# Expert loop of a two-block kernel: rows gathered and turned for two experts at a time, small matmuls in four groups, the last chunk of gate and up unsplit

## The chip, the cores and the metric

The kernel runs on one core of a Trainium2 chip. Times are microseconds (us) of device time for one execution. The core has TensorE (PE; the loading of its stationary operand is listed as PEld), VectorE (DVE), ScalarE (ACT), GpSimd (POOL) and SyncE (SP), and 16 DMA engines. The metric is the time of the whole kernel.

## The reference

The input is 512 tokens of width 1024 in fp32. A first block runs a gated convolution and a forgetting attention, then a mixture of experts; a second block runs a chunkwise mLSTM with pooling and a latent attention. The change touches the mixture of experts alone:

```python
def hier_moe(h, w_router_group, w_router_expert, w_e_gate, w_e_up, w_e_down):
    # per token: the best of 4 groups, then the best 2 of its 8 experts, with weights
    ...
    x_rows = hf[row_tok].reshape(n_blocks, MOE_BLOCK, D)

    def expert_block(args):
        xb, e = args
        a = xb @ w_e_gate[e]
        u = xb @ w_e_up[e]
        return (jax.nn.silu(a) * u) @ w_e_down[e]
```

There are 32 experts. Gate and up are 1024x512, down is 512x1024, each 2 MB in fp32. The 512 tokens give 1024 rows in all, 32 per expert on average.

## The kernel before

Each engine runs its own program; semaphores order them. Everything outside the experts is the same in both kernels.

**Precision.** Products run as fp32r matmuls on split operands. ACT copies a weight into an fp32r tile (`gate_hi`, `up_hi`, `down_hi`), DVE subtracts it from the weight (`gate_lo`, `up_lo`, `down_lo`, L2257, in place of the loaded weight), each in two halves of 128x2048. The tokens of an expert, at most 64 (`CAP`), are the stationary operand `xs`, with the high parts in columns 0 to 63 and the low parts in columns 64 to 127. For each of the 8 chunks of 128 input features PE runs `xs` against the high and against the low weights (N = 512), into one bank (L1658 and L1659 for gate, L1615 and L1616 for up).

**Sums.** The two halves of rows of a product are added, and turned at once, by 8 small plain fp32 matmuls against `twice` (L1634), after ACT has copied the banks to `g_sb` and `u_sb`. silu, the product `hx` (DVE L2281), its split into `hxs` and the down product (L1682) follow; ACT and DVE add its two halves to `ys` (L2292), and POOL scatters the rows to `y_dram`.

**Rows.** POOL gathers an expert's 64 rows from `h2_dram` into `xg[p]` with an indirect DMA (L771), by a column of `table` that it first copies into `get_row[p]` (L782). Unused places hold an index out of bounds. PE turns them with 8 transposes (L1588) into bank 0, and ACT (`x_high`) and DVE (`x_low`, L2276) split them into `xs[p]`.

**Order.** `period(e, p)` is written out for each engine, with p = e mod 2, and loops run over pairs of experts. On PE it is gate of e, among whose chunks the sums of e - 1 and the turning of the rows of e + 1 are spread one by one, then up of e, then down of e - 1. On ACT: silu of e - 1, first half of gate_hi of e + 1, hxs of e - 1, g_sb of e, x_high of e + 1, second half of gate_hi, u_sb of e, up_hi of e + 1, y_low of e - 1, down_hi of e. On DVE: hx and hxs of e - 1, first half of gate_lo of e + 1, x_low of e + 1, second half, up_lo of e + 1, ys of e - 1, down_lo of e. POOL waits for the turned rows of e + 1, gathers those of e + 3 and scatters those of e - 1.

**Loads.** Gate, up and down have two buffers each (`ring_gate` and so on). SP asks for gate of e + 2 when gate of e is done (`next_gate`, L644), in the same way for up (L648) and, one period later, for down (L652). All go through one queue. The high tiles have one buffer only, so ACT starts gate_hi of e + 1 when gate of e is done.

After expert 31 POOL gives `moe_done` when the last scatter has landed, SP loads the rows of `y_dram` back, and the second block begins.

Of the kernel before, what the change touches and what calls it, by code (L numbers as in the profile page):

```python
# [37 lines left out]
CAP = 64  # L38
TOPK = 2
# [177 lines left out]
def build_kernel(nc, t):  # L217

    with ExitStack() as ctx:
# [14 lines left out]
        bank = [ctx.enter_context(nc.psum_tensor(f"bank{i}", [P, 512], F32)) for i in range(8)]  # L234
# [32 lines left out]
        get_row = [misc(f"get_row{p}", [CAP, 1], I32) for p in range(2)]  # L267
# [59 lines left out]
        xg = [at(f"xg{p}", [CAP, D], F32, BASE + 2 * BIG + 4096 * p) for p in range(2)]  # L327
# [251 lines left out]
        gathered = [sem(f"gathered{p}") for p in range(2)]  # L579
# [10 lines left out]
        half_rows = lambda x: slice(64 * x, 64 * x + 64)  # L590

# [148 lines left out]
        def _(pool):  # L740
# [18 lines left out]
            for p in range(2):  # L759
                step(nc.gpsimd.memset(ys[p][:, :], 0.0))  # L760
                if p == 1:
                    step(nc.gpsimd.memset(xg[p][:, :], 0.0))
                pool.dma_start(y_dram[TOPK * SEQ:, :], ys[p][:, :]).then_inc(scattered, 16)
                pool.wait_ge(scattered, 16 * (p + 1))
# [5 lines left out]
            def gather(p):  # L770
                pool.indirect_dma_start(out=xg[p][:, :], out_offset=None, in_=h2_dram,  # L771
                                        in_offset=bass.IndirectOffsetOnAxis(ap=get_row[p][:, :], axis=0),
                                        bounds_check=SEQ - 1, oob_is_err=False).then_inc(gathered[p], 16)
# [6 lines left out]
            def get(e, p):  # L780

                nc.gpsimd.tensor_copy(get_row[p][:, :], table[:, bass.ds(each(e, 1), 1), 0]).then_inc(sem("get_ready"), 1)  # L782
                pool.wait_ge(sem("get_ready"), each(e, 1, 1))
                pool.sem_inc(turn, 1)
                gather(p)
# [11 lines left out]

            get((None, 0), 0)
            get((None, 1), 1)
            for e in range(2):  # L800
                pool.wait_ge(x_turned, e + 1)
                get((None, e + 2), e)
            with pool.Fori(0, NE // 2 - 1) as i:
                for k in range(2):
                    e, p = (i, 1 + k), (1 + k) % 2
                    pool.wait_ge(x_turned, each(e, 1, 2))
                    pool.sem_inc(turn, 1)
                    get(expert(e, 3), 1 - p)
                    put(expert(e, -1), 1 - p)
            for e in range(NE - 2, NE):  # L810
                put((None, e), e % 2)
            for p in range(2):
                pool.wait_ge(gathered[p], 16 * (NE // 2 + 1))
# [4 lines left out]
            with pool.If(count > 0):  # L818
                with pool.Fori(0, OVF) as i:
                    with pool.If(count > i):  # L820
                        pool.wait_ge(sem("ovf_free"), i + 1)
                        pool.sem_inc(turn, 1)
                        nc.gpsimd.tensor_copy(get_row[0][:, :], table[:, bass.ds(i + NE, 1), 0]).then_inc(sem("ovf_rows"), 1)
# [5 lines left out]
                        pool.indirect_dma_start(out=xg[0][:, :], out_offset=None, in_=h2_dram,  # L829
                                                in_offset=bass.IndirectOffsetOnAxis(ap=get_row[0][:, :], axis=0),  # L830
# [26 lines left out]
        def _(act):  # L857
# [197 lines left out]
            def gate_high(e, p, half):  # L1055
# [3 lines left out]
                cs = slice(half * KC // 2, (half + 1) * KC // 2)  # L1059
                copy(gate_hi[:, cs, :], ring_gate[p][:, cs, :]).then_inc(gate_hi_made, 1)  # L1060

            def up_high(e, p):
                act.wait_ge(up_done, each(e, 1))
                act.wait_ge(up_landed[p], each((e[0], e[1] - p), 8, 16))
                for half in range(2):
                    cs = slice(half * KC // 2, (half + 1) * KC // 2)
# [9 lines left out]
            def x_high(e, p):  # L1076
                act.wait_ge(x_turned, each(e, 1, 1))
                copy(xs[p][:, :, 0:CAP], bank[0][:, :].rearrange("p (c n) -> p c n", c=KC)).then_inc(x_hi_made, 1)
# [273 lines left out]
        def _(pe):  # L1352
# [233 lines left out]
            def turn_row(p, c):  # L1586
                rows = xg[p][:, :].rearrange("t (p c) -> t c p", c=KC)
                return pe.transpose(bank[0][:, c * CAP:(c + 1) * CAP], rows[:, c, :], ident[0:CAP, 0:CAP])  # L1588

            def turn_rows(p, done):  # L1590
# [1117 lines left out]
```

## Time and profile before

| | |
|---|---|
| runs | 1952.59 us median of 3 (1952.17 to 1953.96) |
| the profiled execution | 1952.4 us, of which the span is 1950.6 us |
| mean granted TensorE clock | 0.967 |
| PE busy | 1821.7 us, 93% of the span |
| PEld busy | 1490.4 us, 76% |
| DVE busy | 1199.7 us, 62% |
| ACT busy | 1003.1 us, 51% |
| POOL busy | 334.2 us, 17% |
| DMA | 326.49 MB, mean 167 GB/s |

The span runs from the first instruction to the last; the execution's own time has 1.8 us more around it. The expert loop lies between about 642 and 1185 us of the span. Ends of matmuls are modelled, so the starts of two of them say more than a duration. A share of busy DMA engines can come out a little above 1, since packets of two queues overlap on an engine. A line number is that of the kernel before; L866 is ACT's copy helper.

### The profile page before, as it was taken

The numbers are of one execution on the slowest core, as the hardware profiler recorded it, in microseconds if no ns is written. First come the engines' busy times: TensorE is split into PE (matmuls) and PEld (weight loads), VectorE is DVE, ScalarE is ACT, GpSimd is POOL, SyncE is SP. The second block draws the span as 40 slices with busy tenths as digits, with TensorE's granted clock in tenths as the row PEclk, the third lists the DMA queues.
The fourth block names the chain that finished last, engine by engine and source line by source line (L and its number), as shares of the span: only waits on it lengthen the run. The fifth ranks groups of instructions, "written<-read, shape, count | busy, mean of one in ns | idle before, by whom it ended". The sixth has DMA issues, their size and how long they took to land.

```text
span 1950.6 us, 23766 instructions
## 1 busy us (share of the span) xinstructions
PE 1821.7 (93%) x8894; PEld 1490.4 (76%) x8894; DVE 1199.7 (62%) x1641; ACT 1003.1 (51%) x1332; POOL 334.2 (17%) x191
## 2 busy tenths in 40 slices
PE   7999999999898799999999993989999998999898
PEld 6888878888787577777777772868778887878467
DVE  3442435455554899999999995652548633327453
ACT  4222244444513689898989883445333223438331
POOL 0000000000000155555555540100001000000000
PEclk9999999999999799999999996989999999999799
DMA  7755447433146799999999973323022422213001
GB/s 145 104 91 93 107 74 65 70 57 62 44 142 240 277 406 405 403 405 402 403 402 404 401 280 113 113 72 107 1 87 87 152 87 81 87 46 106 6 1 65
DMA packets 129364, 326.49 MB, mean 167 GB/s; under 512 B 8448, under 2 KB 84992, under 8 KB 121088
## 3 DMA queue, kind: packets, MB, share of 16 engines
q1 hardware_dynamic: 123408, 315.85, 50.4%
q0 software_dynamic: 5440, 8.93, 1.4%
q8 instruction: 57, 0.93, 0.2%
q10 hardware_dynamic: 432, 0.56, 0.1%
q14 instruction: 27, 0.22, 0.0%
HBM read 319.02 MB, written 15.21 MB: 171 GB/s over the span
## 4 chain that ended last, share of the span: by engine, by line
PE 60%; DVE 22%; issue 12%; ACT 4%; DMA 1%; DVEq 0%; POOL 0%; SPq 0%; POOLq 0%; ACTq 0%
PE bank L1355 16%; PE bank L1357 15%; PE bank L1356 15%; DVE gate_lo L2257 5%; DVE down_lo L2257 5%; DVE up_lo L2257 4%; PE bank L1431 2%; DVE ys L2292 2%; PE bank L1526 2%; PE bank L1441 1%; PE bank L1882 1%; ACT w_hi L866 1%; PE bank L1797 1%; DVE xs L2276 1%; PE bank L1881 1%
## 5 line engine op out<-in xcount | busy, mean ns | idle before, releaser
L1910 DVE TENSOR_TENSOR w_lo<-w_raw,w_hi 128x2048 fp32r<-128x2048 f32 (+2 forms) x83 | 179.5, 2164 | 341.5 <-ACT w_hi L866 341.3
L866 ACT ACTIVATE w_hi<-w_raw 128x2048 fp32r<-128x2048 f32 (+3 forms) x139 | 182.2, 1332 | 280.8 <-PE bank L1357 81.5
L1355 PE MATMUL bank<-h1T_hi,w_hi 128*128 128x512 f32 x456 | 183.4, 402 | 0.0
L1357 PE MATMUL bank<-h1T_hi,w_lo 128*128 128x512 f32 x456 | 179.4, 393 | 0.0
L1356 PE MATMUL bank<-h1T_lo,w_hi 128*128 128x512 f32 x456 | 178.7, 392 | 0.0
L793 POOL COPY put_row<-table 64x1 int32 (+1 forms) x32 | 122.3, 3823 | 175.7 <-DVE ys L2292 173.5
L2257 DVE TENSOR_TENSOR gate_lo<-gate,gate_hi 128x2048 fp32r<-128x2048 f32 x64 | 146.0, 2284 | 0.0
L2257 DVE TENSOR_TENSOR up_lo<-up,up_hi 128x2048 fp32r<-128x2048 f32 x64 | 143.6, 2285 | 1.1 <-ACT up_hi L866 1.1
L2257 DVE TENSOR_TENSOR down_lo<-down,down_hi 128x2048 fp32r<-128x2048 f32 x62 | 138.8, 2276 | 0.0
L866 ACT ACTIVATE gate_hi<-gate 128x2048 fp32r<-128x2048 f32 x64 | 122.4, 1914 | 9.3 <-DMA h_dram<-h_tok 9.3
L1658 PE MATMUL bank<-gate_hi,xs 128*128 128x512 f32 x248 | 120.2, 485 | 0.9 <-DVE gate_lo L2257 0.9
L866 ACT ACTIVATE up_hi<-up 128x2048 fp32r<-128x2048 f32 x64 | 119.1, 1920 | 0.0
L866 ACT ACTIVATE down_hi<-down 128x2048 fp32r<-128x2048 f32 x62 | 114.9, 1904 | 0.0
L1355 PE MATMUL bank<-h2T_hi,w_hi 128*128 128x512 f32 x264 | 103.0, 390 | 3.3 <-DVE hy_t L2467 2.2
L1615 PE MATMUL bank<-up_hi,xs 128*128 128x512 f32 x256 | 104.7, 409 | 0.0
L1357 PE MATMUL bank<-h2T_hi,w_lo 128*128 128x512 f32 x264 | 102.7, 389 | 0.0
L1356 PE MATMUL bank<-h2T_lo,w_hi 128*128 128x512 f32 x264 | 102.7, 389 | 0.0
L1616 PE MATMUL bank<-up_lo,xs 128*128 128x512 f32 x256 | 101.5, 396 | 0.0
L1357 PEld LDWEIGHTS bank<-h1T_hi,w_lo 128*128 128x128 f32 x456 | 86.1, 189 | 18.5
L1355 PEld LDWEIGHTS bank<-h1T_hi,w_hi 128*128 128x128 f32 x456 | 87.0, 191 | 16.3
L1356 PEld LDWEIGHTS bank<-h1T_lo,w_hi 128*128 128x128 f32 x456 | 86.4, 189 | 16.6
L1659 PE MATMUL bank<-gate_lo,xs 128*128 128x512 f32 x248 | 98.1, 395 | 0.0
(490 smaller groups left out, 4351.5 us busy)
## 6 DMA issues: line engine op xcount, KB each, us to landing
gate<-in_w_e_gate SPq DMA_DIRECT2D x32, 2048.0 KB, 12.3
up<-in_w_e_up SPq DMA_DIRECT2D x32, 2048.0 KB, 14.5
down<-in_w_e_down SPq DMA_DIRECT2D x32, 2048.0 KB, 16.1
w_raw<-in_w_in SPq DMA_DIRECT2D x24, 1024.0 KB, 9.8
w_raw<-in_a_w_in SPq DMA_DIRECT2D x20, 1024.0 KB, 5.2
w_raw<-in_w_in SPq DMA_DIRECT2D x16, 512.0 KB, 9.6
w_raw<-in_a_w_out SPq DMA_DIRECT2D x8, 1024.0 KB, 4.9
w_raw<-in_c_w_in SPq DMA_DIRECT2D x6, 1024.0 KB, 5.3
```

The lines of the kernel that those rows point to most:

```text
L793: nc.gpsimd.tensor_copy(put_row[p][:, :], table[:, bass.ds(each(e, 1), 1), 1]).then_inc(sem("put_ready"), 1)
L866: return nc.scalar.activation(out, in_, ACT.Copy, scale=scale)
L1355: pe.matmul(out, sh, mh, start=start, stop=False)
L1356: pe.matmul(out, sh, ml, start=False, stop=False)
L1357: return pe.matmul(out, sl, mh, start=False, stop=stop)
L1431: ins = pe.transpose(out[0:src.shape[-1], at_:at_ + n], src, ident)
L1615: pe.matmul(out[:, :], x[:, c, :], wh[:, c, :], start=c == 0, stop=False)
L1616: ins = pe.matmul(out[:, :], x[:, c, :], wl[:, c, :], start=False, stop=c == KC - 1)
L1658: pe.matmul(bank[2][:, :], xs[p][:, c, :], gate_hi[:, c, :], start=c == 0, stop=False)
L1659: ins = pe.matmul(bank[2][:, :], xs[p][:, c, :], gate_lo[p][:, c, :], start=False, stop=c == KC - 1)
L1910: V.tensor_tensor(ring_view(w_lo, n), ring_view(raw, n), ring_view(w_hi, n).bitcast(F32), ALU.subtract)\
L2257: V.tensor_tensor(lo[:, cs, :], raw_[:, cs, :], hi[:, cs, :].bitcast(F32), ALU.subtract).then_inc(lo_made_, 1)
```

## The change

1. **Rows by pairs.** `xg` and `get_row` become one tile of 128 partitions each, for two experts: 0 to 63 for the even one, 64 to 127 for the odd one. One indirect DMA gathers both. PE turns the pair with 8 transposes of 128x128 (`turn_pair`) into a tile of two banks, `turned`, in every other period (p = 1); `turned_of(x)` is the view of one expert's columns. ACT and DVE still split the rows of one expert per period. POOL waits once per pair, gathers the pair after next, and then scatters two experts' outputs.
2. **Small matmuls in four groups.** In `gate_among` the sums, and the transposes where there are any, follow every second chunk, two at a time, in place of one after each chunk.
3. **Last chunk unsplit.** Chunk 7 of gate and up (`SPLIT_KC` = 7) is no longer split. The second halves of gate_hi, up_hi, gate_lo and up_lo cover 3 chunks of 4, and PE runs one plain fp32 matmul against the loaded weight in place of two fp32r ones. down is as before.

```diff
+SPLIT_KC = KC - 1
...
+        turned = ctx.enter_context(nc.psum_tensor("turned", [P, 1024], F32))
+        bank = [turned[:, 512 * (i // 3):512 * (i // 3) + 512] if i in (0, 3)
...
+        turned_of = lambda x: turned[:, :].rearrange("p (c n) -> p c n", c=KC)[:, :, half_rows(x)]
...
+            def get_pair(e):
+
+                for x in range(2):
+                    nc.gpsimd.tensor_copy(get_row[half_rows(x), :], table[:, bass.ds(each(expert(e, x), 1), 1), 0])\
+                        .then_inc(sem("get_ready"), 1)
+                pool.wait_ge(sem("get_ready"), each(e, 1, 2))
                 pool.sem_inc(turn, 1)
-                gather(p)
+                gather()
...
+            get_pair((None, 0))
+            pool.wait_ge(x_turned, 1)
+            get_pair((None, 2))
             with pool.Fori(0, NE // 2 - 1) as i:
+                pool.wait_ge(x_turned, i + 2)
+                pool.sem_inc(turn, 1)
+                get_pair((i, 4))
                 for k in range(2):
...
+                    put((i, k), k)
...
-                cs = slice(half * KC // 2, (half + 1) * KC // 2)
+                cs = slice(half * KC // 2, min(half * KC // 2 + KC // 2, SPLIT_KC))
...
+                if p == 0:
+                    act.wait_ge(x_turned, e[1] // 2 + 1 if e[0] is None else e[0] + (e[1] // 2 + 1))
+                copy(xs[p][:, :, 0:CAP], turned_of(p)).then_inc(x_hi_made, 1)
...
+            def turn_pair(c):
+                rows = xg[:, :].rearrange("t (p c) -> t c p", c=KC)
+                return pe.transpose(turned[:, c * P:(c + 1) * P], rows[:, c, :], ident)
...
+            def row_product(out, x, wh, wl, w, c, e, low_made):
+
+                if c % (KC // 2) == 0:
+                    pe.wait_ge(low_made, each(e, 2, 1 + c // (KC // 2)))
+                if c >= SPLIT_KC:
+                    return pe.matmul(out[:, :], x[:, c, :].bitcast(F32), w[:, c, :], start=False, stop=c == KC - 1)
+                pe.matmul(out[:, :], x[:, c, :], wh[:, c, :], start=c == 0, stop=False)
+                return pe.matmul(out[:, :], x[:, c, :], wl[:, c, :], start=False, stop=c == KC - 1)
...
+                    ins = row_product(bank[2], xs[p], gate_hi, gate_lo[p], ring_gate[p], c, e, gate_lo_made)
                     if c == KC - 1:
                         ins.then_inc(gate_done, 1)
...
+                    if c == 1:
                         sum_waits(expert(e, -1))
...
+                        if turn_next:
+                            turn_waits(expert(e, 1))
+                    if c % 2 == 1:
+                        for k in (c - 1, c):
+                            ins = sum_of(k)
...
+                        if turn_next:
+                            for k in (c - 1, c):
+                                ins = turn_pair(k)
...
             def period(e, p):
-                gate_among(e, p)
+                gate_among(e, p, turn_next=p == 1)
...
+            pe.wait_ge(gathered, 16)
+            for c in range(KC):
+                ins = turn_pair(c)
+            ins.then_inc(x_turned, 1)
             gate_product((None, 0), 0)
-            turn_x((None, 1), 1)
             up_both((None, 0), 0)
...
-                cs = slice(half * n, half * n + n)
+                cs = slice(half * n, min(half * n + n, SPLIT_KC))
```

## Rows read from the trace of the kernel before

**Rows 1.** Stretches: length; busy us of PE, PEld, DVE, ACT, POOL; clock; DMA; GB/s

```profile
660.00:692.40 32.40, 31.47 (x141) 24.64 (x140) 31.29 (x21) 28.98 (x27) 8.09 (x5) 1.00 0.93 354
692.40:1114.70 422.30, 422.30 (x1873) 332.91 (x1873) 409.70 (x287) 384.92 (x352) 242.42 (x106) 1.00 1.01 403
1131.00:1150.40 19.40, 19.40 (x87) 15.43 (x86) 18.92 (x14) 17.32 (x16) 11.61 (x6) 1.00 0.72 292
1164.80:1171.60 6.80, 6.80 (x25) 5.93 (x25) 4.45 (x4) 2.17 (x3) 0.00 (x0) 0.50 0.42 136
```

**Rows 2.** DMA queues in 692.4 to 1114.7: packets, MB, share of 16 engines

```profile
q1 hardware_dynamic: 21165, 163.32, 96.4%
q0 software_dynamic: 4160, 6.89, 5.0%
```

**Rows 3.** Two gate loads and the next to last down load: issue, and us to landing

```profile
L644 SPq DMA_DIRECT2D gate<-in_w_e_gate x1: 351/351/351, 671.5 to 671.5; - x1
DMA to landing us min/median/max: 8.6/8.6/8.6
...
L644 SPq DMA_DIRECT2D gate<-in_w_e_gate x1: 338/338/338, 1126.0 to 1126.0; - x1
DMA to landing us min/median/max: 14.6/14.6/14.6
...
L652 SPq DMA_DIRECT2D down<-in_w_e_down x1: 379/379/379, 1134.2 to 1134.2; - x1
DMA to landing us min/median/max: 16.2/16.2/16.2
```

**Rows 4.** Groups by line in 692.4 to 1114.7: busy us, mean ns, idle before

```profile
L2257 DVE TENSOR_TENSOR gate_lo<-gate,gate_hi 128x2048 fp32r<-128x2048 f32 x53 | 121.0, 2284 | 0.0
...
L866 ACT ACTIVATE gate_hi<-gate 128x2048 fp32r<-128x2048 f32 x53 | 101.5, 1914 | 0.0
...
L2276 DVE TENSOR_TENSOR xs<-bank,xs 128x512 fp32r<-128x512 f32 x26 | 17.8, 684 | 0.0
```

**Rows 5.** DVE in order of time, one expert: start, length, line

```profile
848.28 4.48 DVE L2257 TENSOR_TENSOR down_lo<-down,down_hi 128x2048 fp32r<-128x2048 f32 x2
...
864.52 4.47 DVE L2257 TENSOR_TENSOR down_lo<-down,down_hi 128x2048 fp32r<-128x2048 f32 x2
...
869.81 0.43 DVE L2286 TENSOR_TENSOR hxs<-hx,hxs 128x256 fp32r<-128x256 f32 x1 [0.48 <-ACT hxs L866]
```

**Rows 6.** PE in order of time: gate steps with a turn, then in the last gate

```profile
863.19 0.50 PE L1658 MATMUL bank<-gate_hi,xs 128*128 128x512 f32 x1
...
864.27 0.50 PE L1658 MATMUL bank<-gate_hi,xs 128*128 128x512 f32 x1
...
1151.51 0.48 PE L1658 MATMUL bank<-gate_hi,xs 128*128 128x512 f32 x1
...
1152.20 0.48 PE L1658 MATMUL bank<-gate_hi,xs 128*128 128x512 f32 x1
```

**Rows 7.** Plain fp32 matmuls and 128x128 transposes elsewhere: timeline, group, timeline

```profile
1360.63 4.48 PE L1783 MATMUL bank<-q2T,k2T 128*128 128x512 f32 x16
...
L1783 PE MATMUL bank<-q2T,k2T 128*128 128x512 f32 x16 | 7.5, 592 | 0.0
...
1450.03 2.24 PE L1431 MATMUL bank<-const,hm_tok 128*128 128x128 f32 x19
```

**Rows 8.** POOL's groups in the loop, and the first gather in the chain

```profile
L793 POOL COPY put_row<-table 64x1 int32 x26 | 104.6, 4022 | 134.8 <-DVE ys L2292 134.8
L771 POOL DMA_INDIRECT xg<-h_dram,get_row x26 | 71.3, 2742 | 22.1 <-POOL get_row L782 22.1
...
643.72 4.18 DMA xg<-h_dram,get_row
```

**Rows 9.** The tail in order of time: hx of expert 30, first sum of 31

```profile
1161.23 0.41 DVE L2281 TENSOR_TENSOR hx<-sg,bank 128x256 f32<-128x256 f32 x1
...
1164.47 1.66 PE L1634 MATMUL bank<-twice,g_sb 128*128 128x64 f32 x8 [4.84 <-ACT u_sb L866]
```

More of the change, by code:

```diff
@@ L266, in build_kernel @@
         table = misc("table", [CAP, NBLK, 2], I32)
-        get_row = [misc(f"get_row{p}", [CAP, 1], I32) for p in range(2)]
+        get_row = misc("get_row", [2 * CAP, 1], I32)
         put_row = [misc(f"put_row{p}", [CAP, 1], I32) for p in range(2)]
@@ L326, in build_kernel @@
         g_ffn = temp("g_ffn", 2, (P, D))
-        xg = [at(f"xg{p}", [CAP, D], F32, BASE + 2 * BIG + 4096 * p) for p in range(2)]
+        xg = at("xg", [2 * CAP, D], F32, BASE + 2 * BIG)
         ys = [at(f"ys{p}", [CAP, D], F32, BASE + 2 * BIG + 8192 + 4096 * p) for p in range(2)]
@@ L578, in build_kernel @@
         router_loaded = sem("router_loaded")
-        gathered = [sem(f"gathered{p}") for p in range(2)]
+        gathered = sem("gathered")
         scattered = sem("scattered")
@@ L768, in _, with gather @@
             pool.wait_ge(results, order[("logits", 0)] + 1)
[L770 to L773, printed above, removed]
+            def gather():
+                pool.indirect_dma_start(out=xg[:, :], out_offset=None, in_=h2_dram,
+                                        in_offset=bass.IndirectOffsetOnAxis(ap=get_row[:, :], axis=0),
+                                        bounds_check=SEQ - 1, oob_is_err=False).then_inc(gathered, 16)
             def scatter(p):
@@ L796, in put @@
                 scatter(p)
[L798 to L802, printed above, removed]
+            get_pair((None, 0))
+            pool.wait_ge(x_turned, 1)
+            get_pair((None, 2))
             with pool.Fori(0, NE // 2 - 1) as i:
+                pool.wait_ge(x_turned, i + 2)
+                pool.sem_inc(turn, 1)
+                get_pair((i, 4))
                 for k in range(2):
[L805 to L809, printed above, removed]
+                    put((i, k), k)
             for e in range(NE - 2, NE):
                 put((None, e), e % 2)
-            for p in range(2):
-                pool.wait_ge(gathered[p], 16 * (NE // 2 + 1))
+            pool.wait_ge(gathered, 16 * (NE // 2 + 1))
             pool.wait_ge(scattered, 16 * (NE + 2))
@@ L1608, in down_product, with both_halves @@
                 ins.then_inc(done, 1)
[L1610 removed]
+            def row_product(out, x, wh, wl, w, c, e, low_made):
[5 more added lines that the diff above has]
+                return pe.matmul(out[:, :], x[:, c, :], wl[:, c, :], start=False, stop=c == KC - 1)
+            def both_halves(out, x, wh, wl, w, e, low_made, done):
                 for c in range(KC):
[L1613 to L1616 removed]
+                    ins = row_product(out, x, wh, wl, w, c, e, low_made)
                 ins.then_inc(done, 1)
@@ L1624, in gate_product @@
                 gate_waits(e, p)
-                both_halves(bank[2], xs[p], gate_hi, gate_lo[p], e, gate_lo_made, gate_done)
+                both_halves(bank[2], xs[p], gate_hi, gate_lo[p], ring_gate[p], e, gate_lo_made, gate_done)
             def sum_waits(e):
@@ L1686, in up_both @@
             def up_both(e, p):
-                both_halves(bank[4], xs[p], up_hi, up_lo[p], e, up_lo_made, up_done)
+                both_halves(bank[4], xs[p], up_hi, up_lo[p], ring_up[p], e, up_lo_made, up_done)
             def period(e, p):
-                gate_among(e, p)
+                gate_among(e, p, turn_next=p == 1)
                 up_both(e, p)
```

62 lines of the change are left out of this document (18 added, 44 removed).

## The prediction

> **What bounds the kernel now.** The table by stretches was read first [rows 1]. The changed code runs only in the expert loop, from about 642 to 1185 us of the span. In 692.4 to 1114.7, which is 26 experts of 16.24 us, PE is busy all the time, DVE 97% (409.70 of 422.30 us), ACT 91%, and the 16 DMA engines have a share of 1.01 at 403 GB/s. Three resources are full at once, so the question is not which one the change relieves, but which one is left.
>
> DVE is a closed ring: its down_lo halves start 16.24 us apart (848.28, 864.52), and the only idle time inside is 0.48 us for ACT's hxs [rows 5]. Its work is 6 halves of 2.28 us [rows 4] and small things. PE has nothing to spare either. The DMA queue is the third. It moves 163.32 + 6.89 = 170.21 MB in 422.3 us [rows 2], 6.55 MB per expert (three loads of 2.10 MB, and 0.26 MB of gather and scatter). The gate load issued at 671.5 lands 8.6 us later, the one issued at 1126.0 takes 14.6 us [rows 3]. Only at the two ends has it room, with shares of 0.93 and 0.72 [rows 1]. So between them the queue is not merely busy: it falls behind while the engines keep their 16.24 us. Gate loads of experts 3 and 31 land at 680.1 and 1140.6: 460.5 us for 28 experts, **16.45 us each**. Nobody waits for them yet, since the buffers are two deep and the loop began with slack. That slack is almost used up when the loop ends.
>
> **The change part by part.**
>
> *DVE and ACT.* gate_lo and up_lo, second halves, shrink from 2048 to 1536 columns. A 2048-column half takes 2.284 us, the 512-column xs 0.684 us [rows 4]: 1.04 ns per column, so 0.53 us saved; in proportion it would be 0.57. Twice per expert: 1.07 to 1.14. DVE goes from 16.24 to 15.1 us. ACT loses a quarter of a 1.914 us copy twice, at most 0.96, and is no bound before or after.
>
> *PE, turns.* One chunk step of gate with a turn in it takes 864.27 - 863.19 = 1.08 us; in the last gate, which turns nothing, 1152.20 - 1151.51 = 0.69 [rows 6]. A turn costs 0.39, eight of them 3.1 us per expert. Afterwards there are 8 per two experts, 128 rows by 128. Transposes of that form run at (2.24 - 0.27)/18 = 0.11 us [rows 7] when nothing has to be switched; the old place's 0.39 is the upper bound. I take 0.11 to 0.2, so 0.9 to 1.6 per two experts. Grouping by two halves the changes between kinds, which I count at nothing (below nothing is possible, 0.1 per change). Saved: about 2.5 us per expert.
>
> *PE, last chunk.* A step of 0.69 us without a turn is the two split matmuls and a sum of two small instructions; at 0.11 each the sum leaves 0.47 for the pair. The pair becomes one plain fp32 matmul of 128x512, two instructions. In the kernel before, 16 such instructions with 5120 columns take 4.48 us [rows 7], 0.87 ns per column, hence 0.9 us for 2 x 512 columns; two mean durations of 0.592 bound it at 1.18. Taking 0.9: +0.43, twice per expert, +0.9 (at most +1.4). PE goes from 16.24 to about 14.6. With both upper bounds it is 16.24 - 1.55 + 1.4 = 16.1, still less than the queue's 16.45 below: off the path.
>
> *POOL.* Per two experts one wait, two row copies, one indirect DMA of 128 rows, and then both scatters, which now queue behind it. A copy is at most 4.02 us, the indirect issue 2.74 for 64 rows and at most twice that, its landing some 10 us behind [rows 8]: 8 + 0.9 + 5.5 + 10 = 24 us after the turn. The rows are needed two experts later, some 28 us after the turn. The slack of 4 is smaller than it was but stays; the scatters have a whole expert to spare. Cost nothing; if that cover were gone, PE's next gate would wait with its sums behind it.
>
> *What is late next.* The engines could now do an expert in 15.1 us. The queue cannot: it needs 16.45. Starting from 8.6 us, landing times grow by 16.45 - 15.1 = 1.35 per expert, until a gate load takes two experts (32.9) less what lies between its landing and gate_done (1.9 hi, 2.3 lo, the other half, x, the product: 12 to 13), thus about 20 us. That is reached after 9 experts, near 810 us. From there on the engines wait for loads, and each expert takes what the queue takes. The 1.1 us that DVE gains per expert, 33 us in all, is not paid out.
>
> **The sum.** What remains is the tail. Before, the load of down for expert 30 lands at 1134.2 + 16.2 = 1150.4 [rows 3], but DVE, working through its ring, starts hx of expert 30 only at 1161.23, 10.8 us later; the rest of the chain (sums, two downs, two scatters) hangs on that hx [rows 9]. Paced by loads, DVE is only as far behind as its own work: hi half 1.9, then, since up_lo and the 1.27 us of ys are still in front, two lo halves 4.5, and about 0.3 of hand-overs: 6.7 us. Gain 4.1. The load of down for 31 can be asked for earlier than 1150.4, so it does not take its place.
> Two terms move the landings. At the start the first gather carries 128 rows instead of 64 (4.18 us to land before [rows 8]) and the turn is twice as wide, but the second turn (1.1 us) between gate and up is gone: the request at 671.5, from which the queue never idles again, comes 0.3 earlier to 1.3 later; I take 0.5 later. Then the pace. By bytes alone the queue would need 6.55 MB / 403 GB/s = 16.25 us; landings, which wait for the slowest of 16 engines, show 16.45. So some engines carry 0.20 us more per expert than the mean. Gather and scatter are the only traffic that need not be even (half of each table's rows are unused). A gather of 128 rows may spread them differently: if the unevenness went altogether it would be worth 28 x 0.20 = 5.6 us, if it grew by a quarter it would cost 1.4. Nearest to no effect, but not at it, I take 1.4 gained.
> Sum: 1952.4 (the profiled execution's own time: span 1950.6 and 1.8 around it; the median of the runs is 1952.59, the same within 0.01%) - 4.1 + 0.5 - 1.4 = 1947.4; I say **1947.5**. Own range of this case: 1941 to 1952.
>
> **Rivals.** Measurements of this kernel tell about 0.2% (3.9 us) from no change.
> 1. *The queue is not at its limit*: 403 GB/s is only what was asked, and it gives more when asked sooner. Then DVE sets the pace: 30 x 1.1 = 33 us and the tail, about 1919. For it: the demand at 16.24 us is 403 too. Against: share 1.01 throughout, and landing times that grow, which a queue with room does not show. Chance 0.07. The Trainium skill, in "DMA: Bandwidth & Descriptors", section on specifications, has a fabric ceiling of 435 GB/s, by which an estimate of 15.1 us per expert follows, just this rival, and beside it an HBM limit of about 358, which the 403 here already exceeds.
> 2. *Slower: the clock falls in the new waits.* PE idles about 16.4 - 14.6 = 1.8 us per expert, most of it in one piece before down. At 1164.8 to 1171.6 the granted clock was 0.50 [rows 1], and before it PE had waited 4.84 us for u_sb [rows 9]. Such a stretch in each expert loses 3.4 us of PE work: 14.6 + 3.4 = 18.0, which is 1.6 over the queue, for some 20 experts: about 1980. It decides once more than 2 x 1.8 = 3.6 us per expert run at half clock. Against: the wait is under half of the one shown. Chance 0.09.
> 3. *Nothing reaches the end*: the last loads land later by as much as the tail saves (more start delay, scatters held up), 1952. Chance 0.08.
> The forecast has 0.76.
>
> **How the numbers follow.** Of the 0.76, about 0.72 lies below 1948.7, 0.28 within 0.2%. Faster: 0.55 + 0.07 = 0.62. Same: 0.21 + 0.08 = 0.29. Slower: 0.09. The range 1940 to 1954 holds the forecast's range and rival 3; rivals 1 and 2 are left out.
>
> **What the profile after would show.** DVE busy 14.7 us per expert and PE idle 2 us of 16.3, the loop's experts still 16.3 to 16.45 us apart on average although the first ten are near 15.2; waits of ACT's gate_hi, up_hi and down_hi for DMA, absent before; landing times of gate, up and down all near 20 us from 810 on; DMA share still 1.01; turns at about 0.11 to 0.2 us; hx of expert 30 near 1157. Wrong would be: 15.2 us per expert to the end (rival 1), a clock under 1.00 between 692 and 1114 (rival 2), PE waiting for the gather, or a down_lo that ends more than 8 us behind its landing.

## The result, and the profile after

| | before | changed |
|---|---|---|
| median of the runs | 1953.28 us (1952.17 to 1954.30, 4 runs) | 1930.25 us (1929.72 to 1933.07, 4 runs) |
| the profiled execution | 1952.4 us | 1929.7 us, span 1927.6 |
| DVE busy | 1199.7 us | 1167.0 us |
| POOL busy | 334.2 us | 233.0 us |

The ratio is 0.9881, with a 95% interval of 0.9868 to 0.9893: **faster by 23 us**, where 5 had been forecast. The whole gain is made in the expert loop: hx of expert 30 starts at 1138.29, against 1161.23 [rows 9], 22.9 us earlier.

The stretches of the changed kernel answer to [rows 1] (length; busy us of PE, PEld, DVE, ACT and POOL; clock; DMA share; GB/s). The second and third are the body of the loop:

```profile
660.00:692.40 32.40, 29.25 (x136) 21.98 (x135) 29.19 (x21) 29.25 (x28) 8.65 (x5) 1.00 0.97 368
692.40:900.00 207.60, 197.92 (x939) 153.14 (x939) 200.41 (x151) 190.48 (x184) 90.07 (x49) 1.00 1.01 422
900.00:1080.00 180.00, 165.32 (x772) 127.55 (x771) 168.97 (x126) 160.76 (x156) 59.12 (x41) 0.99 1.01 421
```

The DMA share is 1.01 as before, but the same share now moves 421 to 422 GB/s and not 403. So the share doesn't show how fast the packets were.

Four gate loads answer to [rows 3] (issue, us to landing), and the down load of expert 30:

```profile
L648 SPq DMA_DIRECT2D gate<-in_w_e_gate x1: 352/352/352, 671.7 to 671.7; - x1
DMA to landing us min/median/max: 8.0/8.0/8.0
...
L648 SPq DMA_DIRECT2D gate<-in_w_e_gate x1: 333/333/333, 883.9 to 883.9; - x1
DMA to landing us min/median/max: 18.8/18.8/18.8
...
L648 SPq DMA_DIRECT2D gate<-in_w_e_gate x1: 339/339/339, 1103.9 to 1103.9; - x1
DMA to landing us min/median/max: 17.5/17.5/17.5
...
L656 SPq DMA_DIRECT2D down<-in_w_e_down x1: 379/379/379, 1113.4 to 1113.4; - x1
DMA to landing us min/median/max: 18.1/18.1/18.1
```

Landings grow from 8.0 to 18.8 us in the first 14 experts and stay there: the queue falls behind until the engines wait for it. The chain that ended last shows the change of regime (start, us, what):

```profile
839.76 2.28 DVE down_lo L2266
854.93 2.27 DVE down_lo L2266
862.91 2.28 DVE up_lo L2266 x2
873.66 3.99 PE bank L1689 x16
883.91 18.83 DMA gate<-in_w_e_gate
905.55 5.54 PE bank L1689 x16
921.95 3.74 PE bank L1689 x16
925.85 18.86 DMA down<-in_w_e_down
```

Up to 883.91 it runs through DVE's ring, whose experts are 15.17 us apart (down_lo at 852.73 and 867.90); from there on it runs through loads. The list of waits in 692.4 to 1080 (us in total, times, longest) has what [rows 4] had none of:

```profile
ACT down_hi L868 <- DMA down<-in_w_e_down: 13.9, 13, 1.5
...
ACT gate_hi L868 <- DMA gate<-in_w_e_gate: 7.5, 7, 1.6
```

So the regime of the forecast came: DVE first, then the queue. Only the queue was faster than forecast.

### The profile page after: what moved, and what is told of

Read it like the earlier page. It is cut to its first block, busy times and chain, and to the rows that moved or that the text cites. A ratio compares the mean times of both kernels' runs of the same rounds, so it can differ in the third digit from the quotient of the medians.

```text
span 1927.6 us, 23396 instructions
## 1 busy us (share of the span) xinstructions
PE 1770.0 (92%) x8766; PEld 1441.4 (75%) x8766; DVE 1167.0 (61%) x1641; ACT 977.0 (51%) x1332; POOL 233.0 (12%) x174
## 4 chain that ended last, share of the span: by engine, by line
PE 63%; DVE 13%; DMA 9%; issue 9%; ACT 6%; DVEq 0%; POOL 0%; SPq 0%; ACTq 0%; POOLq 0%
PE bank L1358 12%; PE bank L1360 12%; PE bank L1359 12%; DMA down<-in_w_e_down 6%; PE turned L1358 3%; PE turned L1360 3%; PE turned L1359 3%; DVE down_lo L2266 3%; PE bank L1689 2%; DVE gate_lo L2266 2%; DVE up_lo L2266 2%; PE bank L1529 2%; PE bank L1434 1%; PE bank L1444 1%; ACT w_hi L868 1%
## 5 line engine op out<-in xcount | busy, mean ns | idle before, releaser
L1358 PE MATMUL bank<-h1T_hi,w_hi 128*128 128x512 f32 x376 | 152.4, 405 | 0.0
L1360 PE MATMUL bank<-h1T_hi,w_lo 128*128 128x512 f32 x376 | 148.2, 394 | 0.0
L1359 PE MATMUL bank<-h1T_lo,w_hi 128*128 128x512 f32 x376 | 147.6, 392 | 0.0
L2266 DVE TENSOR_TENSOR gate_lo<-gate,gate_hi 128x2048 fp32r<-128x2048 f32 x64 | 128.9, 2017 | 0.0
L2266 DVE TENSOR_TENSOR up_lo<-up,up_hi 128x2048 fp32r<-128x2048 f32 x64 | 126.5, 2019 | 1.1 <-ACT up_hi L868 1.1
L799 POOL COPY put_row<-table 64x1 int32 (+1 forms) x32 | 86.3, 2696 | 261.0 <-DVE ys L2301 258.8
L1689 PE MATMUL bank<-down_hi,hxs 128*128 128x512 f32 x248 | 83.3, 418 | 28.9 <-DVE hxs L2295 28.8
L1620 PE MATMUL bank<-gate_hi,xs 128*128 128x512 f32 x224 | 97.7, 436 | 3.3 <-DVE gate_lo L2266 1.8
L1689 PEld LDWEIGHTS bank<-down_hi,hxs 128*128 128x128 f32 x248 | 45.6, 193 | 62.3 <-DVE hxs L2295 32.4
L1360 PEld LDWEIGHTS bank<-h1T_hi,w_lo 128*128 128x128 f32 x376 | 71.1, 189 | 15.6
L1358 PE MATMUL bank<-h2T_hi,w_hi 128*128 128x512 f32 x200 | 78.2, 391 | 3.3 <-DVE hy_t L2476 2.2
```

The source lines that it names most:

```text
L799: nc.gpsimd.tensor_copy(put_row[p][:, :], table[:, bass.ds(each(e, 1), 1), 1]).then_inc(sem("put_ready"), 1)
L1358: pe.matmul(out, sh, mh, start=start, stop=False)
L1359: pe.matmul(out, sh, ml, start=False, stop=False)
L1360: return pe.matmul(out, sl, mh, start=False, stop=stop)
L1620: pe.matmul(out[:, :], x[:, c, :], wh[:, c, :], start=c == 0, stop=False)
L1689: ins = pe.matmul(bank[6 + a][:, :], hxs[:, f, :], w[:, f, a * 512:(a + 1) * 512], start=f == 0 and w is down_hi, stop=f == FC - 1 and w i ...
```

## The experiments

Each was compared with the kernel before on its own chip; ratios are to that kernel. Where two experiments ran on different chips, their ratios say more than the difference of their times. Three questions were asked in turn.

### Which part brings the gain?

**Parts 1 and 2 alone** (pair gather, pair turn, four groups; all chunks split):

```diff
-SPLIT_KC = KC - 1
+SPLIT_KC = KC
```

> The changed kernel with all 8 chunks split again, so that only the pair gather, the pair turn and the four groups are left. DVE then has 16.24 us of work per expert. Theory A (the pair gather raised the queue's ceiling from about 403 to 421 GB/s): DVE's 16.24 us set the pace, about 1950, the packets of 4096 bytes short, landings flat instead of growing. Theory B (the ceiling was always near 421 and the queue of the kernel before only followed what was asked): about 1950 too, 403 GB/s, landings grow as before. Theory C (fewer and shorter ACT and DVE reads of the weights made the packets quicker): landings grow as before. In all three the turns' saving on PE is worth nothing by itself, since DVE is the ring: 1948 to 1953.

Measured: 1957.2 us median of 10 runs (1953.3 to 1959.8), ratio 1.0012 (1.0003 to 1.0022). No gain, and even a trace of a loss. DVE's down_lo halves start 16.24 us apart (856.04, 872.28), and PE idles (busy 163.6 of 180 us in 900 to 1080, at a clock of 0.92), which costs nothing while DVE sets the pace. But the gate loads no longer fall behind: over the loop they land in 8.4, 10.2 and 12.8 us (least, median, most). The kernel before asks at the same pace of 16.24, and its gate loads take 8.8 us at 785.1 and 16.2 at 980.0. That was the first sign that the queue itself had changed.

**Part 3 alone**: the kernel before, with the last chunk of gate and up unsplit on ACT, DVE and PE, in the old order:

```diff
+                    if c >= SPLIT_KC:
+                        ins = pe.matmul(out[:, :], x[:, c, :].bitcast(F32), w[:, c, :], start=False, stop=c == KC - 1)
```

> The kernel before with only the last chunk of gate and up unsplit. DVE needs 15.2 us per expert. On PE the plain chunk takes 0.85 us in place of 0.47, twice per expert, and the eight turns per expert stay: if PE's 16.24 us of the kernel before were all work, it now needs 17.0, 30 x 0.76 = 23 us more, 1975; if they held up to 0.5 us of slack per expert that the profile can't show, 1960. A rival says that PE had a whole us of slack per expert and DVE's ring sets the pace here too: 1930 to 1935.

Measured: 1970.3 us, ratio 1.0081 (1.0061 to 1.0100): **slower**. down_lo starts at 853.46 and 870.32, 16.86 us apart, with PE busy in all of 900 to 1080:

```profile
900.00:1080.00 180.00, 180.00 (x770) 137.34 (x769) 157.07 (x117) 146.76 (x144) 76.69 (x43) 1.00 1.01 388
```

DVE has room here (157 of 180 us), and PE has none: nearly all of its 16.24 us before were work. The parts don't add: one alone is worth nothing, the other costs 16 us, both together gain 23. Note the share: 1.01 here too, at 388 GB/s, while gate loads land in 8.8 us (median), so this queue is plainly not full. **A share of 1.01 is no sign of a full queue.** Landings that grow are one.

### Was the old queue at its limit, and what is it about the gathers?

**The old arrangement with room on every engine.** In the kernel before, chunk 7 of gate and up is left out on ACT, DVE and PE (the products miss it). Loads and gathers stay:

```diff
+                    if c < SPLIT_KC:
                         pe.matmul(out[:, :], x[:, c, :], wh[:, c, :], start=c == 0, stop=False)
```

> The kernel before with chunk 7 of gate and up left out on ACT, DVE and PE (the product misses that chunk); loads, gathers of 64 rows, turns and their places are as before. All engines are then free to run at about 15.3 us per expert, so this asks the old queue for more. Theory A (its ceiling with single gathers is 16.2 to 16.45 us per expert): 1943 to 1950 at 400 to 406 GB/s, with engines waiting for loads. Theory B: about 1925 to 1932 at 420 GB/s or more, landings near 19 us late in the loop. Theory C, since ACT and DVE read as little as in the changed kernel: the same as B.

Measured: 1947.0 us, ratio 0.9957 (0.9936 to 0.9978). It is the forecast's course to the letter: gate loads land in 8.4 us at 672.7 and in 18.7 at 794.2, and from 810.4 to 1073.8 sixteen experts take 263.4 us, **16.46 us each**, with ACT waiting:

```profile
ACT down_hi L867 <- DMA down<-in_w_e_down: 32.0, 18, 2.4
```

The old queue's limit was real, and the forecast's 16.45 met it. In the changed kernel it isn't there. ACT and DVE read as little in both, so their traffic (theory C) is out. POOL's timeline has a gather:

```profile
725.14 2.21 POOL L772 DMA_INDIRECT xg<-h_dram,get_row  x1 [0.85 <-POOL get_row L783]
```

and stretches of one microsecond each show what follows (last number GB/s):

```profile
730.00:731.00 1.00, 1.00 (x8) 0.78 (x6) 1.00 (x3) 1.00 (x2) 0.00 (x0) 1.00 1.33 496
731.00:732.00 1.00, 1.00 (x6) 0.79 (x5) 1.00 (x2) 1.00 (x1) 0.00 (x1) 1.00 1.03 324
732.00:733.00 1.00, 1.00 (x6) 0.81 (x5) 1.00 (x1) 0.98 (x2) 1.00 (x1) 1.00 0.87 315
733.00:734.00 1.00, 1.00 (x8) 0.75 (x6) 1.00 (x2) 0.61 (x1) 1.00 (x1) 1.00 0.73 303
734.00:735.00 1.00, 1.00 (x5) 0.82 (x5) 1.00 (x1) 0.93 (x2) 1.00 (x1) 1.00 0.95 389
```

From 6 us after the start of the gather's issue all DMA traffic runs at three quarters of its speed for 3 us. The kernel before has the same dip, 6 us behind its gather issued at 857.1:

```profile
863.00:864.00 1.00, 1.00 (x6) 0.79 (x5) 1.00 (x3) 1.00 (x2) 0.00 (x0) 1.00 1.08 332
864.00:865.00 1.00, 1.00 (x6) 0.83 (x5) 1.00 (x2) 1.00 (x1) 0.00 (x0) 1.00 0.94 295
```

In the changed kernel there is no such dip at the same distance behind a pair gather, issued at 710.3:

```profile
715.00:716.00 1.00, 1.00 (x4) 0.62 (x4) 1.00 (x3) 1.00 (x2) 0.00 (x0) 1.00 0.98 401
716.00:717.00 1.00, 1.00 (x7) 0.77 (x6) 1.00 (x2) 1.00 (x1) 0.26 (x1) 1.00 1.02 402
717.00:718.00 1.00, 1.00 (x6) 0.80 (x5) 1.00 (x1) 0.98 (x3) 1.00 (x1) 1.00 1.03 397
718.00:719.00 1.00, 1.00 (x6) 0.78 (x5) 1.00 (x2) 1.00 (x1) 1.00 (x1) 1.00 1.00 401
```

Single slices of a microsecond jump (496 at 730 above; 340 in the changed kernel at 714, with a DMA share of 0.80), so all gathers issued between 700 and 1080 were averaged too. In the 3 us that begin 5 us behind the issue, the traffic was 314 GB/s in the kernel before (23 gathers), 352 in the one without chunk 7 (24), and 412 in the changed kernel (13). The GB/s of 866.3 to 1028.7, cut into 40 slices, show one dip per expert in the kernel before, and none in the changed one:

```profile
GB/s 437 408 430 342 431 405 436 343 416 420 431 326 430 427 423 333 438 424 429 328 433 405 438 324 442 409 434 314 427 428 436 326 441 416 443 350 437 392 416 351
...
GB/s 410 404 437 424 424 405 443 428 408 407 438 431 410 415 435 428 402 425 437 422 403 428 433 416 407 418 445 427 402 427 425 421 409 439 428 409 418 428 426 400
```

**Only the gather's DMA undone.** The changed kernel, its pair of experts gathered by two DMAs of 64 rows:

```diff
-                pool.indirect_dma_start(out=xg[:, :], out_offset=None, in_=h2_dram,
-                                        in_offset=bass.IndirectOffsetOnAxis(ap=get_row[:, :], axis=0),
+                for x in range(2):
+                    pool.indirect_dma_start(out=xg[half_rows(x), :], out_offset=None, in_=h2_dram,
+                                            in_offset=bass.IndirectOffsetOnAxis(ap=get_row[x][:, :], axis=0),
```

> The changed kernel with each pair's rows asked for by two indirect DMAs of 64 rows, one behind the other, each with an index tile of its own; all else as changed. Theory A1 (a 64-row gather slows the whole queue for some 3 us, whoever asks for it: 0.9 us per expert): experts 16.2 to 16.4 us apart once the loads are late, 1943 to 1948, and each pair of gathers shows a dip of the GB/s. Theory A3 (not the gather's shape, but the old turns and their places): as the changed kernel, 1930, 421 GB/s without dips.

Measured: 1949.9 us median of 10, ratio 0.9975 (0.9961 to 0.9989). About four fifths of the gain are gone with this one edit. The queue is back at 403 GB/s in 900 to 1080, and its dips are there, twice per pair:

```profile
745.00:746.00 1.00, 1.00 (x6) 0.55 (x5) 1.00 (x3) 1.00 (x1) 0.00 (x0) 1.00 1.08 340
746.00:747.00 1.00, 1.00 (x6) 0.85 (x6) 1.00 (x1) 0.97 (x3) 0.83 (x1) 1.00 0.96 336
747.00:748.00 1.00, 1.00 (x6) 0.79 (x5) 1.00 (x2) 1.00 (x1) 1.00 (x1) 1.00 0.96 397
748.00:749.00 1.00, 1.00 (x6) 0.82 (x5) 1.00 (x1) 0.69 (x1) 1.00 (x1) 1.00 1.08 352
749.00:750.00 1.00, 1.00 (x5) 0.47 (x3) 1.00 (x1) 0.00 (x0) 1.00 (x1) 1.00 0.80 217
```

One of the two writes partitions 0 to 63, the other 64 to 127: it isn't the place. Turns, groups and POOL's copies are those of the changed kernel: it isn't they (theory A3).

**No gathers at all** in the loop, on the old arrangement with chunk 7 left out (rows of experts 2 and 3 are turned again and again):

```diff
-                gather(p)
+                if e[0] is None:
+                    gather(p)
```

> The same old arrangement with chunk 7 left out, and in the loop no gathers at all (the rows of experts 2 and 3 are turned again and again); POOL's copies, the turns and the scatters stay. If the gathers are what holds the queue at 16.4 us per expert (theories A1 and A2): no dips, 420 GB/s or more is to be had, 6.42 MB per expert need 15.2 us, so DVE's ring sets the pace and landings stay under 15: 1920 to 1926. If something else in the old arrangement does (A3): 1942 to 1948.

Measured: 1920.7 us, ratio 0.9817 (0.9793 to 0.9841), 423 GB/s in 900 to 1080, no wait of ACT for a load. As expected: in the old arrangement the gathers cost at least 26 us (1947.0 - 1920.7, on two chips; 27 by the ratios; DVE's ring is the bound now), of which bytes (0.13 MB at 421 GB/s, 0.31 us, times 28) explain 9 us.

**Width, and where the used rows lie.** Two kernels on the old arrangement with chunk 7 left out. In the first each gather, still one per expert, is 128 rows wide with the upper 64 out of bounds. In the second the upper 64 repeat the lower, so that twice the rows move, half of them in partitions 0 to 31, half in 64 to 95:

```diff
-        xg = [at(f"xg{p}", [CAP, D], F32, BASE + 2 * BIG + 4096 * p) for p in range(2)]
+        xg = [at(f"xg{p}", [P, D], F32, BASE + 2 * BIG + 4096 * p) for p in range(2)]
...
# first kernel
+                step(nc.gpsimd.memset(get_row[p][CAP:, :], 8 * SEQ))
# second kernel
+                for x in range(2):
+                    nc.gpsimd.tensor_copy(get_row[p][half_rows(x), :], table[:, bass.ds(each(e, 1), 1), 0]).then_inc(sem("get_ready"), 1)
```

> The kernel of the last experiment on the old arrangement (chunk 7 of gate and up left out on the engines, rows gathered expert by expert), but each gather's DMA is 128 rows wide: its upper 64 indices are out of bounds, so bytes, used rows and number of DMAs stay. Theory A2 (the shape of 64 partitions does it): no dips, 420 GB/s, experts at DVE's 15.2 us and later at about 15.5, 1925 to 1930. Theory A1 in its other form (each gather DMA costs, however wide, or 32 rows landing in partitions 0 to 31 do it): 1945 to 1949 as without the widening.

> The old arrangement with chunk 7 left out and 128-row gathers, one per expert, as before, but the upper 64 indices now repeat the lower 64: used rows lie in partitions 0 to 31 and 64 to 95, as in the changed kernel's pair gather, at the price of 0.13 MB more per expert. Theory U (with 32 used rows packed at one end some DMA engines get more rows than others, fall behind, and the whole queue runs at their pace): the even spread wins more than the bytes cost, experts about 15.9 us apart late in the loop instead of 16.4, 1933 to 1938. Theory N (what counts is the number of gather DMAs, one per expert or one per two): nothing won, bytes lost: 16.7 us apart, 1948 to 1956.

Measured: 1944.4 us, ratio 0.9942 (0.9924 to 0.9961), and 1940.8 us, 0.9944 (0.9923 to 0.9965), on two chips: by the ratios the two are equal, though the second moves more bytes, and neither is clear of the 64-row gathers' 0.9957. Neither theory had both right: the first kernel has no dips behind its gathers, as A2 said, and nearly A1's time; the second lies between U and N. The stretches of the first:

```profile
700.00:840.00 140.00, 138.82 (x623) 110.52 (x621) 133.36 (x100) 126.58 (x123) 76.94 (x38) 1.00 1.02 421
900.00:1080.00 180.00, 169.29 (x746) 132.01 (x746) 162.42 (x121) 153.82 (x148) 57.51 (x44) 1.00 1.00 399
```

and of the second:

```profile
700.00:840.00 140.00, 138.83 (x621) 110.39 (x619) 133.03 (x100) 126.18 (x123) 76.86 (x47) 1.00 1.02 421
900.00:1080.00 180.00, 172.54 (x762) 134.81 (x760) 165.60 (x123) 155.51 (x151) 63.27 (x55) 1.00 1.01 419
```

Widening alone brings the queue from 404 (same stretch, 64-row gathers) to 421 GB/s in the early part: the dips go with the width (406 and 418 GB/s in the same 3 us behind 24 gathers each). But once the loads are late, the first falls to 399, and the second, with more bytes, keeps 419. The first has dips of another kind then, 13 to 14 us behind gathers issued at 960.6 and 977.2:

```profile
974.00:975.00 1.00, 1.00 (x6) 0.77 (x6) 1.00 (x2) 0.17 (x1) 1.00 (x2) 1.00 0.72 279
...
991.00:992.00 1.00, 1.00 (x6) 0.80 (x5) 1.00 (x1) 0.99 (x3) 1.00 (x2) 1.00 0.69 291
```

So there are **two effects**: a 64-row gather slows all packets while it runs, and in a wide gather used rows packed at one end cost speed. The landings show the second one early, too: with the same bytes per expert, the same 421 GB/s and DVE's same 15.17 us, the gate load issued at 823.2 takes 18.7 us in the first kernel and 14.8 in the changed one. The second effect fits DMA engines that get more rows than others and fall behind, while the others run dry. The Trainium skill, "DMA: Bandwidth & Descriptors", section on the descriptor swizzle, gives partitions 0 to 31 of a 128-partition transfer to engines 0 to 7, four each, and 64 to 95 to engines 8 to 15; it names no gather there. By it the first kernel's used rows sit on half of the engines and the second's on all. The two kernels' 399 and 419 agree with that; no row here names an engine, so it is not shown. Against it: the 64-row gathers, whose used rows lie in partitions 0 to 31 as well, have no such late dips (between 900 and 1080, in the 6 us from 12 us behind each issue, 416 GB/s on average, where the first kernel has 380 and the second 424). The second kernel moves 9 us of bytes more than the changed one; without them it would be at about 1932, by this estimate near the changed kernel's 1930.

**More rows in a 64-row gather**: no index out of bounds (unused places fetch row 511), otherwise the old arrangement with chunk 7 left out:

```diff
+            step(V.tensor_scalar(slot_g[:, :], slot_g[:, :], float(SEQ - 1), None, ALU.min))
             V.tensor_copy(table[:, :, 0], slot_g[:, :]).then_inc(sem("table_made"), 1)
```

> The old arrangement with chunk 7 left out and 64-row gathers, in which no index is out of bounds any more (an unused place fetches row 511): 64 rows instead of 32 per gather, 0.13 MB more per expert. If the packing of the used rows at one end is what costs (theory U): the even spread pays for the bytes, 15.9 to 16.2 us per expert, 1935 to 1942. If a 64-row gather slows all packets while it runs (theory S): the slow stretch doubles with the rows, 16.9 us per expert or more, 1955 to 1965.

Measured: 1969.0 us, ratio 1.0085 (1.0068 to 1.0102), 396 GB/s late in the loop. All 64 places are used here, so packing can't be what costs, and it is 22 us slower than with 32 rows (25 by the ratios), 0.79 us per expert, of which the bytes are 0.31. That is theory S in kind, and above its 1955 to 1965: the 3 us behind the issue fall from 352 to 334 GB/s, less than a stretch twice as long. That half of the places ask for one and the same row may add to it; this was not tested.

### What bounds the changed kernel?

**Less work on its engines**: chunks 6 and 7 of gate and up left out. Beside it, the same **without gathers** in the loop:

```diff
-SPLIT_KC = KC - 1
+SPLIT_KC = KC - 2
...
                 if c >= SPLIT_KC:
-                    return pe.matmul(out[:, :], x[:, c, :].bitcast(F32), w[:, c, :], start=False, stop=c == KC - 1)
+                    return None
...
# second kernel
-                gather()
+                if e[0] is None:
+                    gather()
```

> The changed kernel with chunks 6 and 7 of gate and up left out on ACT, DVE and PE; loads as they are. The engines could do an expert in about 14.1 us. If the changed kernel's queue is at its own limit (421 GB/s, 15.5 us per expert) from about 900 us on, this gains next to nothing: landings reach 19 us by the sixth expert, then 15.5 us apart to the end, 1926 to 1933. If the queue gives what is asked: 14.1 us per expert, about 1895.

> The changed kernel with chunks 6 and 7 left out and no gather in the loop (the rows of the first pairs are turned again and again). Its queue is the bound, so this prices the pair gather: if it costs no more than its bytes (0.13 MB at 421 GB/s, 0.31 us per expert), experts are 15.2 us apart instead of 15.5 and the time is about 1920. If the pair gather has a cost of its own beyond bytes, the time falls further, to 1912 or less.

Measured: 1928.5 us, ratio 0.9855 (0.9830 to 0.9880), and 1914.5 us, 0.9811 (0.9794 to 0.9828). Engines that need 1 us less per expert gain nothing clear of noise against the changed kernel (next paragraph): it is bound by its queue. The pair gathers cost 14 us by the times and 9 by the ratios (the two ran on different chips), some 9 of them bytes. So 0 to 5 are their own, against 17 or more in the old arrangement.

**The changed kernel once more**, on the second one's chip:

> The changed kernel once more, on the chip of this call, since the kernel before spreads wider here than in the first comparison (1951 to 1962). It should again be 1929 to 1933, with 421 GB/s; if it isn't, part of what the other experiments show belongs to the chip and not to the kernels.

Measured: 1928.6 us, ratio 0.9875 (0.9859 to 0.9892), 422 and 421 GB/s as in its first profile.

**A faster queue.** down is loaded with one row of 16 KB per partition; in the first kernel the sums pick the matching columns of g_sb and u_sb, in the second ACT sorts them when it copies the banks; the third has two chunks unsplit in addition:

```diff
-            down_src = lambda e: t["w_e_down"][bass.ds(e, 1)].rearrange("e (c p) n -> p (e c) n", p=P)
+            down_src = lambda e: t["w_e_down"][bass.ds(e, 1)].rearrange("e (p c) n -> p (e c) n", p=P)
...
# first kernel
-                return pe.matmul(bank[1][:, k * CAP:(k + 1) * CAP], src[:, f * P:(f + 1) * P], twice[:, :], start=True, stop=True)
+                return pe.matmul(bank[1][:, k * CAP:(k + 1) * CAP], src[:, :].rearrange("t (q f) -> t f q", f=FC)[:, f, :], twice[:, :], start=True, stop=True)
# second and third
-                copy(g_sb[:, :], bank[2][:, :]).then_inc(gate_out, 1)
+                copy(g_sb[:, :].rearrange("t (f q) -> t f q", f=FC), bank[2][:, :].rearrange("t (q f) -> t f q", f=FC)).then_inc(gate_out, 1)
```

> The changed kernel with the inner features of the experts dealt out otherwise: partition p holds features 4p to 4p + 3 of down in place of p, p + 128, ..., so that its load reads one row of 16 KB per partition and not four of 4 KB; the sums pick the matching columns. In the changed kernel a stretch in which almost only 4 KB packets ran (918.5 to 921.5 us) moved 406 GB/s, one with mostly 16 KB packets (909 to 912) 433: 2.1 MB of down would take 4.84 us in place of 5.17. If the queue is the bound of the changed kernel, 0.33 us less per expert: late in the loop 15.2 us apart instead of 15.5, and landings that grow slower: 28 x 0.25 = 7 us, 1921 to 1926. If the picked columns (16 bytes apart) make the loads of the stationary operand slower, PE's gate step grows by 8 x 0.1 us or so, which PE's idle time covers. Rival: the small packets cost nothing once the queue is mixed, 1928 to 1930.

> As the last experiment (down loaded in rows of 16 KB), but ACT sorts the columns when it copies the banks to g_sb and u_sb, so that PE loads contiguous operands again. In the last one the landings stayed at 10 to 12 us, and PE was busy all the time: a group of four sums took 0.73 us in place of 0.39, 1.4 us per expert. If the queue is what bounds the changed kernel late in its loop, then with PE back at 14.2 us the loop goes at DVE's 15.17 us to its end, landings stay under 15 us, ACT waits for no load: 1920 to 1924. If the changed kernel's late 15.5 us have another cause: 1928 to 1931. ACT's strided copies may cost some tenths of a us, twice per expert, which its idle time covers.

> The same with two chunks of gate and up unsplit (SPLIT_KC = 6): DVE 14.1 us per expert, PE 14.2 + 0.76 = 15.0. If the queue needs 15.2 us per expert with rows of 16 KB (6.55 MB at 430 GB/s), it is the bound again: landings grow to 19 us and 1919 to 1923, nothing over the version with one chunk. If it gives more, PE sets the pace at 15.0: 1915 to 1918.

Measured: 1935.5 us (0.9909, 0.9892 to 0.9925), **1925.2 us (0.9851, 0.9835 to 0.9868)** and 1929.7 us (0.9881, 0.9864 to 0.9897).

The first is slower than the changed kernel, for a reason that PE's idle time had been expected to cover. In order of time on PE (start, us), a group of two sums (four instructions) takes 870.82 - 870.09 = 0.73 us:

```profile
870.09 0.92 PE L1644 MATMUL bank<-twice,g_sb 128*128 128x64 f32 x4
870.82 0.48 PE L1620 MATMUL bank<-gate_hi,xs 128*128 128x512 f32 x1
```

In the changed kernel it is 0.37 (863.34 to 863.71). Four such groups cost 1.4 us per expert, PE had only about 1 us of room, and is now busy in all of 700 to 1080. A stationary operand whose columns lie 16 bytes apart is that much slower to use.

The second takes this away and is the fastest of all: 427 GB/s, and ACT's waits for loads fall from 21.6 us to 11.7:

```profile
900.00:1080.00 180.00, 168.69 (x793) 129.73 (x792) 172.11 (x130) 163.74 (x159) 75.24 (x42) 1.00 1.01 427
```

It gains about 5 us on the changed kernel's 1930 (across chips; the intervals of the ratios, 0.9835 to 0.9868 and 0.9868 to 0.9893, just touch), less than hoped: landings still reach 18 us by 960. The third brings the waits back (21.1 us for down, 13.0 for gate, 6.0 for up) and gains nothing, against 1919 to 1923 expected; on the same chip it is 4 us slower than the second. In the profiles hx of expert 30 starts at 1135.48 and 1135.88, so with these loads too the queue is the bound, and the 4 us lie outside the loop or between runs; their cause is open.

## Why the prediction was wrong

Its course was right, one term of its sum was mis-sized. Step by step:

- **DVE 15.1 us per expert**: right. The shortened halves take 1.75 us; the ring is 15.17.
- **PE about 14.6**: right. The plain chunk takes 853.23 - 852.38 = 0.85 us (0.9 forecast). A gate group with two turns takes 848.66 - 847.16 = 1.50 us and one without 863.71 - 862.41 = 1.30: 0.1 us per turn (0.11 to 0.2 forecast). PE idles about 1 us per expert.
- **POOL costs nothing**: right. In the loop PE never waits for xg.
- **The queue becomes the bound, landings near 20 us, then the engines wait**: right, at 884 us and not at 810, since the queue was faster.
- **The tail, 4.1 us**: right. The load of down for 30 lands at 1113.4 + 18.1 = 1131.5, and hx of 30 follows 6.8 us later (6.7 forecast; 10.8 before).
- **The start, 0.5 us later**: 0.2 (671.7 against 671.5).
- **The clock**: 1.00 and 0.99 in the loop; rival 2 did not come.
- **The pace, 1.4 us gained**: here it failed. Gate loads of experts 3 and 31 land at 679.7 and 1121.4: 441.7 us against 460.5, **18.8 us gained**. 1952.4 - 4.0 + 0.2 - 18.8 = 1929.8, and the profiled execution took 1929.7. With the pair gathered by two DMAs the same two landings are 679.3 and 1138.4, 459.1 us apart: 17.4 of the 18.8 us go back with that one edit.

The failed step is the one that sized what a gather of 128 rows does to the queue: "Gather and scatter are the only traffic that need not be even", and hence at most "28 x 0.20 = 5.6 us" to be won. It took the 403 GB/s as what the queue can do and looked for the gathers' cost only in what lies above that, in the 0.20 us of unevenness. The 403 were themselves the result of gathers: an average over some 420 between them and 314 in the 3 us that one runs. The experiments bear this out: 16.46 us per expert with 64-row gathers and room on every engine, and a return to 1950 us (1946.7 in the profiled execution, where 1947.5 had been forecast) when the changed kernel's gather alone was split in two. The forecast is that of the changed kernel with its old gathers. The bound "if the unevenness went altogether" was no bound on the gathers' effect. By bytes alone they are 0.31 us per expert; leaving them out was worth at least 0.9.

Rival 1 (1919, the queue follows demand) had the right sign and the wrong mechanism. Its argument "it gives more when asked sooner" is refuted by the kernel without chunk 7 in the old arrangement, which asked sooner and got 405. The Trainium skill's ceiling of 435 GB/s, cited there ("DMA: Bandwidth & Descriptors", specifications), stands above every longer stretch here, 428 at most. The Trainium skill's swizzle rule, weighed at 2.8 us, pointed at the right operation, but only at one of the two effects.

A second reading was loose and did no harm: the pace was taken from two landings at the ends of the loop. Between them the old gate loads landed in 8.8 us (785.1), 16.2 (980.0) and 14.6 (1126.0): flat at first, then growing, then falling again. A line through the ends hides that, and that its 16.45 met the 16.46 of the kernel without chunk 7 is in part luck.

What stays open: why a 64-row gather slows the packets of the other queue. The width of the transfer does it, not its partitions and not the number of gathers (one wide gather per expert has no dip behind it); scatters of 64 rows, alone in the loop without gathers, left the queue at 423 GB/s. How much of the changed kernel's gain is width and how much is the even place of the used rows was not separated there. The two kernels with wide gathers show that width alone is not enough; how much the place is worth rests on one profile of each.

## What to carry to other kernels

A mean GB/s at a busy share near 1 is not a queue's capacity: cut it into slices of a microsecond and look for what stands at the dips, before taking the mean as a limit. A small indirect DMA can cost far more than its bytes, by slowing every transfer beside it, so try it wider, and with its used rows spread (here the width is shown, the spread less surely). And when three resources are full at once, parts that are worthless or harmful alone can pay together: find which part makes room for which.

## What the runs showed of the hardware

- An indirect gather of 64 rows into SBUF, 32 of them used, holds the whole of the DMA traffic at 314 to 352 GB/s for 3 us (means of 23 and 24 gathers); one of 128 rows doesn't (412, mean of 13). Once the loads are late, an expert takes 16.46 us with the first and 15.6 with the second (14 experts between the landings at 902.7 and 1121.4).
- The packets' share stays at 1.00 to 1.02 from 388 to 428 GB/s, with gate loads landing in 8.8 us or in 19.
- Loads in rows of 16 KB alone moved 427 GB/s, two thirds of them so 421.
- A stationary fp32 operand of 128x128 with columns 16 bytes apart: two sums (four instructions) in 0.73 us and not 0.37. ACT's copy of 128x512 that sorts the same columns takes 0.58 us, as without sorting.
- PE's granted clock late in the loop was 0.93 with chunks 6 and 7 left out (waits for hxs up to 5.0 us), 0.99 in the changed kernel (up to 2.2 us) and 1.00 in the kernel before, where PE never idled. The longest wait alone doesn't order them: with all chunks split it was 0.92, at waits up to 2.9 us, and with two gathers per pair 0.97, at 3.6.
